# Fixed weight buffers and one 8 MB gate/up transfer per expert, from the eighth expert on

## The reference

```
logits = h @ router_w + router_b;  top 4 of 32, softmax over the four
for each expert e, for the rows xb routed to it:
    gu = xb @ w_gu[e] + b_gu[e]            # w_gu[e]: 1024 x 2048
    g = min(gu[:, :1024], 7);  u = clip(gu[:, 1024:], -7, 7)
    a = (u + 1) * (g * sigmoid(1.702 * g))
    y = a @ w_dn[e] + b_dn[e]              # w_dn[e]: 1024 x 1024
    out[token] += y * weight of the token
x = rms_norm(x + out) * final_norm_g
```

## Time and profile before

| | us |
|---|---|
| median of 3 runs (1233.8 to 1235.38) | 1234.9 |
| the profiled execution, its own time | 1233.66 |
| its span, first to last instruction | 1231.9 |
| PE busy in the span | 1176.7 |
| DMA, mean rate over the span | 369 GB/s |
| bytes moved | 455.14 MB |

### The profile page before, as it was taken

How to read it: one execution, slowest core, us unless ns; L and a number is a source line. 1 busy time by engine, 2 the same in 40 slices (tenths; PEclk the granted TensorE clock), 3 DMA queues, 4 the chain that set the end, 5 groups by cost and what they waited for, 6 DMA issues and landing times.

```text
span 1231.9 us, 14292 instructions
## 1 busy us (share of the span) xinstructions
PE 1176.7 (96%) x6223; PEld 606.5 (49%) x6223; DVE 267.6 (22%) x543; ACT 253.2 (21%) x531; POOL 207.7 (17%) x89
## 2 busy tenths in 40 slices
PE   8999999999999999999999999999998989999996
PEld 8989888899433433333343333333333333333332
DVE  3148242232411112111111111121111111111112
ACT  6456455344301011100100100000000000000001
POOL 5865766685100000000000000000000000000000
PEclk9999999999999999999999999999999999999999
DMA  9753544599799999999999999999999999999995
GB/s 316 239 169 123 163 154 137 187 357 387 289 422 438 426 427 428 429 429 429 431 431 429 434 428 431 429 428 433 427 433 427 430 434 424 430 433 427 428 425 235
DMA packets 61127, 455.14 MB, mean 369 GB/s; under 512 B 5017, under 2 KB 33593, under 8 KB 43016
## 3 DMA queue, kind: packets, MB, share of 16 engines
q1 hardware_dynamic: 61064, 454.22, 89.7%
HBM read 453.13 MB, written 1.07 MB: 369 GB/s over the span
## 4 chain that ended last, share of the span: by engine, by line
PE 59%; DMA 37%; DVE 2%; POOL 1%; ACT 1%; issue 0%; DVEq 0%; SPq 0%; ACTq 0%; POOLq 0%
PE ps L546 58%; DMA arena<-in_expert_w_gate_up 34%; DMA arena<-in_expert_w_down 3%; POOL w_parts L535 1%; PE ps L855 1%; DVE arena L1329 0%; DMA arena<-in_mem 0%; PE ps L849 0%; DVE x_normed L1500 0%; PE ps L669 0%; PE ps L553 0%; ACT arena L1045 0%; PE ps L646 0%; DVE arena L1359 0%; DVE arena L1225 0%
## 5 line engine op out<-in xcount | busy, mean ns | idle before, releaser
L546 PE MATMUL ps<-arena,gathered_T 128*64 128x512 f32 x2048 | 475.4, 613 | 37.1 <-DMA arena<-in_expert_w_gate_up 36.9
L546 PE MATMUL ps<-arena 128*64 128x512 f32 (+8 forms) x1650 | 335.7, 534 | 4.1 <-DVE arena L1359 1.6
L546 PEld LDWEIGHTS ps<-arena,gathered_T 128*64 128x64 f32 x2048 | 146.1, 140 | 306.5 <-issue 268.7
L546 PEld LDWEIGHTS ps<-arena 128*64 128x64 f32 (+3 forms) x1650 | 132.2, 153 | 198.8 <-issue 191.5
L535 POOL TENSOR_TENSOR w_parts<-arena,w_parts 128x1024 fp32r<-128x1024 f32 x42 | 103.0, 2474 | 46.8 <-ACT w_parts L1025 37.6
L535 POOL TENSOR_TENSOR w_parts_odd<-arena,w_parts_odd 128x1024 fp32r<-128x1024 f32 x38 | 91.2, 2423 | 45.4 <-ACT w_parts_odd L1025 45.3
L1444 DVE TENSOR_SCALAR arena<-arena 128x128 f32<-128x128 f32 x64 | 19.3, 343 | 318.1 <-PE ps L849 318.1
L1167 ACT COPY arena<-ps 128x256 f32<-128x256 f32 x32 | 11.9, 372 | 361.6 <-PE ps L849 361.6
L1450 DVE TENSOR_SCALAR arena<-ps 128x512 f32<-128x512 f32 x32 | 22.1, 692 | 273.7 <-PE ps L546 273.7
L546 PEld LDWEIGHTS ps<-arena,x_normed 128*128 128x128 f32 x512 | 59.5, 191 | 24.8 <-issue 24.3
L1158 ACT ACTIVATE gathered_T<-ps,g_cols 128x128 f32<-128x128 f32 x128 | 36.6, 369 | 170.2 <-PE ps L546 170.2
(11 more groups left out here) (179 smaller groups left out, 723.3 us busy)
## 6 DMA issues: line engine op xcount, KB each, us to landing
arena<-in_expert_w_gate_up SPq DMA_DIRECT2D x54, 4096.0 KB, 39.4
arena<-in_expert_w_down SPq DMA_DIRECT2D x62, 2048.0 KB, 39.2
arena<-in_expert_w_gate_up SPq DMA_DIRECT2D x20, 2048.0 KB, 13.1
arena<-in_w_in SPq DMA_DIRECT2D x29, 1024.0 KB, 5.3
arena<-in_w_out SPq DMA_DIRECT2D x4, 1024.0 KB, 11.5
arena<-in_expert_w_down SPq DMA_DIRECT2D x4, 1024.0 KB, 41.0
arena<-in_w_mem_kv SPq DMA_DIRECT2D x3, 1024.0 KB, 11.6
arena<-in_w_branch_a SPq DMA_DIRECT2D x2, 1024.0 KB, 5.3
```

The lines of the kernel that those rows point to most:

```text
L546: return nc.tensor.matmul(out, lhsT, rhs, start=start, stop=stop, **kw)
```

## The change

A constant `FIRST_WHOLE` = 7 is added. From expert 7 to expert 30 gate/up is one transfer of 8 chunks (8 MB, 64 KB per partition); expert 31 keeps its four of 2 MB, down keeps its cuts. The slots from there on are fixed: gate/up lies in slots 8 to 15 for experts 7, 9, ..., 31 and in 0 to 7 for 8, 10, ..., 30; down always in slots 16 to 19, but down(31) in 0 to 3. What a transfer has to wait for is worked out by `freed_by`: the last chunk that any of its slots held. The few lines for experts with more than 64 rows, which take slots by their plain number now, do not run on these inputs and are left out.

```diff
+FIRST_WHOLE = 7
@@ transfers()
-        order += [(n, *t) for t in (long if FIRST_LONG <= n < EXPERTS - 1 else short)]
+        whole = [(0, KC)]
+        order += [(n, *t) for t in (short if n < FIRST_LONG or n == EXPERTS - 1 else long if n < FIRST_WHOLE else whole)]
@@
+def ring_slot(c):
+
+    if c < gate_up_chunk(FIRST_WHOLE):
+        return (c + SCORE_SLOT) % RING
+    j = (c - gate_up_chunk(FIRST_WHOLE)) % (2 * EXPERT_CHUNKS)
+    if c >= down_chunk(EXPERTS - 1):
+        return c - down_chunk(EXPERTS - 1)
+    n, j = divmod(j, EXPERT_CHUNKS)
+    return (KC if n == 0 else 0) + j if j < KC else RING - 4 + j - KC
+
+
+def freed_by():
+
+    holds, out = {}, {}
+    for c, (_, _, m) in TRANSFERS.items():
+        slots = range(ring_slot(c), ring_slot(c) + m)
+        out[c] = max(holds.get(r, -1) for r in slots)
+        for a, r in enumerate(slots):
+            holds[r] = c + a
+    return out
@@ SP
-                sp.wait_ge(chunk_used, NF + c - RING + m)
+                sp.wait_ge(chunk_used, NF + FREED_BY[c] + 1)
                 load_weights(*TRANSFERS[c], ring_slot(c))
```

More of the change, by code:

```diff
@@ L171 @@
 TRANSFERS = transfers()
+def ring_slot(c):
[14 more added lines that the diff above has]
+    return out
+FREED_BY = freed_by()
 def last_unit_of(o):
@@ L364, in front_landed @@
             eng.wait_ge(landed[i % FRONT_RING], 16 * (i // FRONT_RING + 1))
-        def ring_slot(c):
-            return (c + SCORE_SLOT) % RING
         def front_fills(r):
@@ L380, in overflow_fills @@
         def overflow_fills(j):
-            return front_fills(ring_slot(j)) + sum(ring_slot(c) == ring_slot(j) for c in TRANSFERS) + 1
+            return front_fills(j) + sum(ring_slot(c) == j for c in TRANSFERS) + 1
         def by_row(dst, tt):
@@ L519, in _ @@
                         for j in range(0, EXPERT_CHUNKS, 2):
-                            load_weights(e_b, j, 2, ring_slot(j))
+                            load_weights(e_b, j, 2, j)
             for tt in range(T):
@@ L972, in _ @@
                             if k % 2 == 0:
-                                pe.wait_ge(landed[ring_slot(k)], (b + overflow_fills(k)) * 16)
-                            gate_up(ring_slot(k), k, XT[:, 0, :, 0:BLK])
+                                pe.wait_ge(landed[k], (b + overflow_fills(k)) * 16)
+                            gate_up(k, k, XT[:, 0, :, 0:BLK])
                             if k == 3:
@@ L984, in _ @@
                             if j % 2 == 0:
-                                pe.wait_ge(landed[ring_slot(j)], (b + overflow_fills(j)) * 16)
-                            down(ring_slot(j), j, 3)
+                                pe.wait_ge(landed[j], (b + overflow_fills(j)) * 16)
+                            down(j, j, 3)
             pe.wait_ge(y_ready, EXPERTS)
```

## The result

The changed kernel takes 1240.62 us (median of 7 runs, 1238.31 to 1243.25), the kernel before 1235.38 us in the same 7 rounds. The ratio is 1.0048, 95% interval 1.0038 to 1.0059: 5 to 6 us slower. The forecast was 1241.4 us. The profiled execution took 1239.16 us, its span is 1237.3.

What follows compares the result with a forecast made beforehand. The prediction took the stream of weights to bound the kernel from step 13 on. Delay 6.2 + clock 0.8 - longer runs 0.5 = 6.5 us took the span from 1231.9 to 1238.4, the median to 1241.4; range 1238.6 to 1244.1.

Steps and rivals of the forecast that it cites:

- The whole transfer as one wait: PE starts a step only when all 8 gate/up chunks are in; free mid-stream, but down(30) starts 6.17 us later.
- The clock: A fall of PE's clock in step 30 adds 1.5 us; at an even chance, 0.8 us is taken.
- Longer runs: Gate/up runs of 64 KB instead of 32 KB: 0.5 us gained, between 1.5 us lost and 2.5 us gained.
- Later issues at the changeover: Gate/up(8) waits for all of down(5), down(7) for down(6); 2.4 us of cover left, so no hole.
- The new wait and its cover: Down(n) waits for PE to use down(n-1); the queue still holds 4.2 us, so the stream keeps share 1.00.
- Faster: Rival, chance 0.05: a transfer's fixed 1.5 us goes in 24 places, 36 us minus 6, about 1205 us.
- Doesn't do what it says: Rival counted inside the forecast's 0.80: a 64 KB row is carried as two of 32 KB; 1242 us.
- Same: Rival, chance 0.10: PE's delay is there, but 64 KB runs are carried faster; about 1236 us.

Runs made afterwards that it cites:

- whole_only_30: The changed kernel's fixed slots and waits, gate/up in halves except expert 30's, one 8 MB transfer: 1242.34 us, ratio 1.0063 to the kernel before.
- whole_to_26: The changed kernel with whole gate/up transfers only for experts 7 to 26, halves for 27 to 30: 1235.15 us, ratio 1.0004 to the kernel before.
- all_short: The kernel before with gate/up of all experts in transfers of 2 chunks, 16 KB runs: 1238.34 us, ratio 1.0031 to the kernel before.
- down_late: The changed kernel, down(6) to down(29) single transfers, 8 to 29 also waiting for the next gate/up's first chunk: 1401.79 us, ratio 1.1348 to the kernel before.
- down_wait3: The changed kernel, first half of down(n), n 8 to 29, waiting for three chunks of down(n-1), not two: 1247.67 us, ratio 1.0103 to the kernel before.
- down_wait4: The changed kernel, down's first half waiting for all four chunks of the down before, still two transfers: 1265.87 us, ratio 1.0253 to the kernel before.
- halves_fixed: The changed kernel's fixed slots and waits, gate/up of experts 7 to 30 again in two transfers of 4 chunks: 1235.67 us, ratio 1.0002 to the kernel before.

## Why the prediction was right

**The whole transfer as one wait.** The places that the prediction named were met within 0.8 us: step 9 at 553.6 (forecast 552.8), step 14 at 700.25 (699.8), step 30 at 1169.52 (1170.2), step 31 at 1193.85 (1194.56), down(30) at 1210.07 (1210.78), no wait behind step 30. The term of 6.17 us measured 5.46, because the stream was 0.7 us earlier; the work of PE from step 30 to down(30) was forecast to the hundredth (40.55 us). One wait before each step, of 1.2 to 3 us, came in 20 of the 22 steps, with 1.0 to 3.4 us. That the delay is free in the middle and paid at the last whole wait was shown by whole_only_30 (all of the cost) and whole_to_26 (none).

**The clock.** An even chance of one fall in step 30: one profile of the changed kernel has none (7.09 us), one has one (8.78 us). The size was 1.7, not 1.5. It can be larger, and the wait before it doesn't set it: 2.9 us after a wait of 10.71 (whole_only_30), 3.0 after one of 2.69 (whole_to_26). That the median came within 1 us of 1241.4 is partly luck, since this term is the mean of two cases and the seven runs lie 5 us apart.

**Longer runs.** Whether the 0.5 us were gained, no run shows: the landing that opens or completes step 30 moves by more than that between executions (1169.52 and 1170.90 in the changed kernel, 1170.23 and 1172.38 with halves). The packet records speak for a small gain: 64 KB took 2425 ns in one packet and 2436 in two, 0.4% on two thirds of the bytes, and 16 KB packets of down took 0.3% longer. The reason that I gave for the value was wrong. "Doubling the run once has moved nothing that the rate can show" rested on one window of 40 us with 431 GB/s. all_short says 4 us over 27 experts. A window of that length can't tell 0.5%.

**Later issues at the changeover.** No hole that costs: 429 GB/s and share 1.00 from 395 to 604 us, with single engines idle for 5 us in all of 3344.

**The new wait and its cover.** The time from the issue of down's first half to the landing of gate/up(n+1) was forecast at 29.4 - 18.35 - 3.5 - 1.6 - 0.2 = 5.75 us with a fall of the clock; it is 1169.52 - 1163.98 = 5.5. The stream did keep its share. But the rule by which I called the rest safe fell: I let the cost begin only when the last of the 16 engines runs dry, 4.2 us away, and priced it at 23 us per us beyond. It begins earlier and gently, 6 us for the first 1.8 us, and then steeply, another 18 us for the next 1.8. The count looked at all engines as one. They end a transfer some us apart, and the early ones run dry first: in the changed kernel that already happens (9 us in the table), without a cost that its rate shows.

Two things in the packet records make up the loss of rate. Against the changed kernel, idle engines are 0.7% more of the engines' time with three chunks and 2.8% with four. And a 16 KB packet with which an engine starts anew takes 1.25 and 1.31 us on average in these two runs, the others 0.62. Over all 16 KB packets the mean is 618 ns in the changed kernel, 633 and 641 in these two, which is another 0.8% and 1.3% on a third of the bytes. Together that is 1.5% and 4.1%; 424 and 412 GB/s are 1.4% and 4.2% under 430.

Why the engines end apart is seen in down_late: the one that carries the instruction packet ends last, 1.7 us behind the middle one, and everything waits for it. In an unbroken stream such a packet comes about once a step too (20 in 561 us in the changed kernel), and it falls on 12 of the 16 engines, as far as the packets can be put in chains. The reading is that there an engine ahead goes on with the next transfer, so that delays of different engines overlap, while behind a stop each delays its own step. No run takes the instruction packets away, so what they cost in down_wait3 and down_wait4 is argued. What is shown is the curve of the four times, that merging down isn't its cause, and how much of the rate goes with idle engines and longer packets.

**The rivals.** "Faster" (36 us by the output's row) didn't come: 24 issues fewer gave nothing with the queue full. The 2.0 us per transfer of the Trainium skill (DMA: Bandwidth & Descriptors, section Anatomy of one DMA), which the page gives for transfers that GpSimd issues while SP issues these, lie beside other data here: halves_fixed, with the 24 transfers more, has a ratio of 1.0002 and whole_to_26, with 20 of them gone, 1.0004. "Doesn't do what it says" is out by the packet count. "Same" by a faster stream is out: 430 GB/s.

## What to carry to other kernels

When one stream of transfers sets the pace, how coarsely it is cut (in runs of 32 KB or more) changes nothing in the middle that these runs can show; what counts is how far the consumer lags behind the stream at the last transfers, because from there on the consumer sets the end. So transfers may be large in the middle, though that gained nothing here, but should be small well before the end: in whole_to_26 PE won back a lag of 9.6 us (between the two halves' landings) to within 1 us from step 26 to step 30, with one fall of the clock on the way.

And keep several microseconds of queued work beyond the point at which the last engine would run dry. By the prediction's count, 4.2 us of it cost nothing in rate, 2.4 us cost 0.5% of the time and 0.7 us cost 2%.

## What the runs showed of the hardware

- A run of 64 KB per partition goes as one packet. Packets of 16, 32 and 64 KB took 615, 1218 and 2425 ns on average; a stream of 16 KB runs alone came to 427 and 428 GB/s, the longer ones mostly to 429 to 431.
- A transfer issued on an empty queue began to move data 1.05 us after its issue (744.93 to 745.98), and the first 16 KB packet of an engine that had been idle took 1.0 to 1.3 us in place of 0.62.
- The 16 engines end a transfer some us apart. Behind a restart the engine that also carried a 16 KB instruction packet was last in 20 of 20 steps, 1.7 us behind the middle one.
- 1.8 us less cover of a full queue cost 0.5% of the time, 3.5 us less cost 2%, with the DMA share still at 1.00 in the first case. The share alone doesn't show that a stream is being disturbed; its GB/s (424) do, and so does the time that single engines are idle.
- The first 32 products behind a fall of the clock took 8.4 to 10.1 us in place of 7.09: 10.05 after a wait of 2.69 us as well as 10.03 after one of 10.71.
